# Interleaved first loads with matmuls on ones ahead of them, and a last pair of output tiles worked by token halves with the final norm beside it

## The reference

```python
# first block: norm, one wide projection
xn = x * rsqrt(mean(x*x) + 1e-6) * norm_w
h = xn @ w_in
...
# last layer of the second block: attention, then SwiGLU, then the final norm
x = x + window_attn_mixer(...)
gu = rmsnorm(x, norm_ffn_w[1]) @ ffn_w_in[1]
x = x + (silu(gate) * up) @ ffn_w_out[1]
return x * rsqrt(mean(x*x) + 1e-6) * norm_final_w
```

## Time and profile before

| | |
|---|---|
| device time, median of 3 runs | 1524.91 us (1524.15 to 1524.92) |
| the profiled execution | 1526.1 us, of which the span of its instructions is 1524.3 us |
| PE busy | 1467.6 us (96% of the span), 7120 instructions |
| DVE, ACT, POOL busy | 833.8, 581.1, 37.8 us |
| DMA | 123.02 MB, mean 81 GB/s |

### The profile page before, as it was taken

One profiled execution on the slowest core, in us unless ns is written; L12 is line 12 of the kernel. 1 busy time (PEld: TensorE's weight loads), 2 busy tenths in 40 slices (PEclk: granted clock), 3 DMA queues, 4 the chain that ended last, 5 costly groups with the idle time before them and its releaser, 6 DMA issues.

```text
span 1524.3 us, 18003 instructions
## 1 busy us (share of the span) xinstructions
PE 1467.6 (96%) x7120; PEld 1199.6 (79%) x7120; DVE 833.8 (55%) x1592; ACT 581.1 (38%) x1032; POOL 37.8 (2%) x43
## 2 busy tenths in 40 slices
PE   6999998999999899999999999999899999999996
PEld 6778795789788678888888887867678888888885
DVE  5677756567645764544345455587755443344433
ACT  5555533354433443322223233366654232222221
POOL 0011000000000000000000000000000000000000
PEclk9999997999999999999999999999999999999998
DMA  6221120032121112222322223210012222322221
GB/s 220 70 83 56 56 83 28 14 116 79 56 83 56 56 59 107 83 93 78 123 107 83 86 83 128 83 56 1 29 55 93 102 86 84 121 94 100 84 81 70
DMA packets 20899, 123.02 MB, mean 81 GB/s; under 512 B 2256, under 2 KB 2896, under 8 KB 9680
## 3 DMA queue, kind: packets, MB, share of 16 engines
q1 hardware_dynamic: 20816, 121.89, 23.2%
HBM read 119.78 MB, written 2.10 MB: 80 GB/s over the span
## 4 chain that ended last, share of the span: by engine, by line
PE 62%; issue 25%; DVE 8%; ACT 4%; DMA 0%; POOL 0%; DVEq 0%; POOLq 0%; SPq 0%; ACTq 0%
PE PS L231 57%; PE PS L246 3%; PE PS L254 2%; DVE WL L219 1%; DVE FT L227 1%; DVE FT L219 1%; ACT FR L206 1%; DVE FR L219 1%; ACT FT L206 1%; ACT WH L206 1%; DVE G L219 1%; DMA RAW<-in_w_in 0%; DVE FT L223 0%; DVE FP L227 0%; DVE STR L227 0%
## 5 line engine op out<-in xcount | busy, mean ns | idle before, releaser
L231 PE MATMUL PS<-XH,WH 128*128 128x512 f32 x1080 | 428.7, 397 | 0.0
L231 PE MATMUL PS<-XH,WL 128*128 128x512 f32 x1080 | 422.1, 391 | 0.0
L231 PE MATMUL PS<-XL,WH 128*128 128x512 f32 x1080 | 421.9, 391 | 0.0
L231 PE MATMUL PS<-FR,WH 128*128 128x512 f32 x1088 | 342.6, 396 | 12.5 <-DVE FR L219 4.8
L219 DVE TENSOR_TENSOR WL<-RAW,WH 128x1024 fp32r<-128x1024 f32 (+2 forms) x242 | 263.2, 1129 | 153.8 <-ACT WH L206 152.9
L206 ACT ACTIVATE WH<-RAW 128x1024 fp32r<-128x1024 f32 (+2 forms) x242 | 223.9, 974 | 141.6 <-PE PS L231 135.0
L231 PEld LDWEIGHTS PS<-FR,WH 128*128 128x128 f32 x1088 | 204.0, 190 | 60.8 <-issue 9.9
L231 PEld LDWEIGHTS PS<-XH,WH 128*128 128x128 f32 x1080 | 203.6, 189 | 48.6 <-issue 7.5
L231 PEld LDWEIGHTS PS<-XH,WL 128*128 128x128 f32 x1080 | 203.4, 188 | 43.4
L231 PEld LDWEIGHTS PS<-XL,WH 128*128 128x128 f32 x1080 | 203.7, 189 | 40.6 <-issue 0.5
L231 PE MATMUL PS<-FR,WL 128*128 128x512 f32 x544 | 214.0, 393 | 0.0
(11 more groups left out here) (114 smaller groups left out, 1274.5 us busy)
## 6 DMA issues: line engine op xcount, KB each, us to landing
RAW<-in_f_in SPq DMA_DIRECT2D x44, 1024.0 KB, 4.8
RAW<-in_w_in SPq DMA_DIRECT2D x13, 1024.0 KB, 4.8
RAW<-in_m_in SPq DMA_DIRECT2D x12, 1024.0 KB, 4.9
RAW<-in_f_oa SPq DMA_DIRECT2D x16, 768.0 KB, 4.3
RAW<-in_f_ob SPq DMA_DIRECT2D x16, 640.0 KB, 3.8
RAW<-in_a_in SPq DMA_DIRECT2D x6, 1024.0 KB, 5.0
RAW<-in_w_out SPq DMA_DIRECT2D x4, 1024.0 KB, 4.9
RAW<-in_m_out SPq DMA_DIRECT2D x4, 1024.0 KB, 4.8
```

Of the source, the lines that this page charges most:

```text
L231: f = lambda e: e.matmul(o, l, r, start=start, stop=stop, skip_group_check=True)
```

## The change

**At the start.** Weight chunk 0 now comes in four pieces of 256 KB, each issued right behind a piece of x of 512 KB. Of the small constants only the eight columns of `norm_w` (4 KB, `n1`) are issued early, the rest (`sm`, 166 KB) behind the last piece. `prep_all` writes out the split of a weight piece and then those of its two x tiles, four times. `warm_up` gives PE 16 matmuls of 128 columns on the tile `ONE` before anything else; their result is not used.

**At the end.** The pairs dp = 0 to 2 are as before. The last pair is `last_pair`: the products for tokens 0 to 255 of both output tiles (66 matmuls of 256 columns), the norm for these tokens, then the same for tokens 256 to 511. Tiles 0 to 5 are multiplied by the final norm weight ahead of that, on ACT, into `G`; tiles 6 and 7 follow by halves. DVE then multiplies four tiles at once by 1/rms (128x4x256), in place, and each such product leaves by one DMA of 512 KB.

```diff
     xv = A["xT"].rearrange("(k p) s -> p k s", p=128)
-    t_sm = load(SM[:, :], A["small"], "sm")
-    t_x = [load(XT[:, 2 * i:2 * i + 2, :], xv[:, 2 * i:2 * i + 2, :], f"x{i}") for i in range(1)]
...
     def w_load(j):
         ap, nk, wdt = chunks[j]
         dst = RAW[:, j % 2, 0:nk * wdt]
         after = w_split[j - 2][-1] if j >= 2 else None
-        if j == 0:
-            half = nk * wdt // 2
-            SP.add(lambda e: e.dma_start(dst[:, 0:half], ap[:, 0:half]), [], (wd[0], 16), 1.5)
-            WHEN[wd[0], 16] = SP.t + 2.0
-            return
-        tok = (wd[j % 2], 16 * (j // 2 + 1))
+        tok = (wd[j % 2], 16 * ((j + 1) // 2))
         SP.add(lambda e: e.dma_start(dst, ap), [after], (wd[j % 2], 16), 3.0)
         WHEN[tok] = SP.t + 2.0
 
-    def w_prep(j, halves=(0, 1)):
...
-        for a, b in [((0, n0), (n0, nk))[i] for i in halves]:
+        for a, b in ((0, n0), (n0, nk)):
             r = RAW[:, j % 2, a * wdt:b * wdt]
-            here = w0b if j == 0 and a else (wd[j % 2], 16 * (j // 2 + 1))
-            toks.append(split(r, WH[:, j % 2, a * wdt:b * wdt], WL[:, j % 2, a * wdt:b * wdt], here, free))
-        if 1 not in halves:
-            w_part[j] = toks
-            return
+            toks.append(split(r, WH[:, j % 2, a * wdt:b * wdt], WL[:, j % 2, a * wdt:b * wdt],
+                              (wd[j % 2], 16 * ((j + 1) // 2)), free))
...
-        n0 = (nk + 1) // 2
-        return j, h, l, [w_split[j][0 if k < n0 else 1] for k in range(nk)]
-    w_load(0)
-    t_x += [load(XT[:, 2 * i:2 * i + 2, :], xv[:, 2 * i:2 * i + 2, :], f"x{i}") for i in range(1, 2)]
-    w0b = load(RAW[:, 0, 1024:2048], chunks[0][0][:, 1024:2048], "w0b")
-    t_x += [load(XT[:, 2 * i:2 * i + 2, :], xv[:, 2 * i:2 * i + 2, :], f"x{i}") for i in range(2, 4)]
+        return j, h, l, [w_split[j][k * len(w_split[j]) // nk] for k in range(nk)]
+    t_x, t_w0, t_n1 = [], [], None
+    for i in range(4):
+        part = slice(512 * i, 512 * i + 512)
+        t_x.append(load(XT[:, 2 * i:2 * i + 2, :], xv[:, 2 * i:2 * i + 2, :], f"x{i}"))
+        t_w0.append(load(RAW[:, 0, part], chunks[0][0][:, part], f"w0{i}"))
+        if i == 0:
+            t_n1 = load(SM[:, 0:8], A["small"][:, 0:8], "n1")
+    t_sm = load(SM[:, 8:NSMALL], A["small"][:, 8:NSMALL], "sm")
     w_load(1)
     w_at[0] = 2
     t_co = load(CO[:, :], A["const"], "co")
...
     def prep_parts(d, wcol):
         w = SM[:, wcol + d:wcol + d + 1]
         x = XT[:, d, :]
-        h = copy(XH[:, d, :], x, st["x"][d], t_sm, st["xfree"], scale=w)
-        l = stt(XL[:, d, :], x, w, XH[:, d, :].bitcast(F32), ALU.mult, ALU.subtract, h, st["x"][d], t_sm, st["xfree"])
+        tw = t_n1 if wcol == C_N1 else t_sm
+        h = copy(XH[:, d, :], x, st["x"][d], tw, st["xfree"], scale=w)
+        l = stt(XL[:, d, :], x, w, XH[:, d, :].bitcast(F32), ALU.mult, ALU.subtract, h, st["x"][d], tw, st["xfree"])
         xs[d] = [h, l]
 
...
+    def warm_up():
+        b, fb = bank.take()
+        for i in range(16):
+            t = mm(PS[:, b, 0:128], ONE[:, :], ONE[:, :], True, True, t_one, fb, last=(i == 15))
+        bank.put(b, t)
     def prep_all(wcol):
-        w_prep(0, (0,))
-        for d in range(KT):
-            prep_parts(d, wcol)
-            if d == 2:
-                w_prep(0, (1,))
+        w_split[0] = []
+        for i in range(4):
+            part = slice(512 * i, 512 * i + 512)
+            w_split[0].append(split(RAW[:, 0, part], WH[:, 0, part], WL[:, 0, part], t_w0[i]))
+            prep_parts(2 * i, wcol)
+            prep_parts(2 * i + 1, wcol)
         for d in range(KT):
             prep_square(d)
...
             if half == 1:
                 st["xfree"] = tu
-            for dp in range(4):
+            for dp in range(3 if half == 1 and next_w == C_FIN else 4):
...
+            if half == 1 and next_w == C_FIN:
+                last_pair(hid)
+                return
             for hh, hl, tk in hid:
                 fr.put(hh, t)
                 fr.put(hl, t)
 
+    def last_pair(hid):
+        YT, oo = G, out.rearrange("(k p) s -> p k s", p=128)
+        cw = lambda d: SM[:, C_FIN + d:C_FIN + d + 1]
+        tm = [copy(YT[:, d, :], XT[:, d, :], st["x"][d], t_sm, st["g", d], scale=cw(d)) for d in range(6)]
+        ws = [w_use(), w_use()]
+        bs = [bank.take(), bank.take()]
+        bn = [bank.take() for _ in range(2)]
+        sq = [ft.take() for _ in range(2)]
+        so = dsem("out")
+        for th in range(2):
+            c = slice(256 * th, 256 * th + 256)
+            done = []
+            for u, (b, fb) in enumerate(bs):
+                for k in range(FH):
+                    j, h, lo, wt = ws[k // 6]
+                    hh, hl, tk = hid[k]
+                    t = mm3(PS[:, b, c], (h[:, k % 6, u * 128:u * 128 + 128], lo[:, k % 6, u * 128:u * 128 + 128]),
+                            (FR[:, hh, c], FR[:, hl, c]), k == 0, k == FH - 1, wt[k % 6], tk, fb, last=(k == FH - 1))
+                done.append(t)
+            (b, fb), rc, m = bn[th], sc(2), sc(2)
+            cols2 = [slice(c.start + 128 * i, c.start + 128 * i + 128) for i in range(2)]
+            for i in range(2):
+                mm(PS[:, b, i:i + 1], ACC[:, cols2[i]], ONE[:, 0:1], i == 0, False, st["acc"], fb, t_one, last=False)
+            for u in range(2):
+                d = 6 + u
+                x = XT[:, d, c]
+                tx = tt(x, x, PS[:, bs[u][0], c], ALU.add, done[u], st["x"][d], xs[d])
+                q, qf = sq[u]
+                t2 = act(FT[:, q, c], x, ACT.Square, tx, qf)
+                tm.append(copy(YT[:, d, c], x, tx, t_sm, st["g", d], scale=cw(d)))
+                for i in range(2):
+                    t = mm(PS[:, b, i:i + 1], FT[:, q, cols2[i]], ONE[:, 0:1], False, u == 1, t2, last=(u == 1 and i == 1))
+            t = ts(m, PS[:, b, 0:2], 1.0 / D, ALU.mult, t, s2=EPS, op1=ALU.add)
+            t = rpow(rc, m, 2, t)
+            for i in range(2):
+                t2 = tr(PS[:, b, 128 + 128 * i:256 + 128 * i], rc[:, i:i + 1].to_broadcast([128, 128]), IDN, t, t_co, last=(i == 1))
+            r = PS[:, b, 128:384].unsqueeze(1).to_broadcast([128, 4, 256])
+            for p in range(2):
+                y = YT[:, 4 * p:4 * p + 4, c]
+                t3 = tt(y, y, r, ALU.mult, t2, tm)
+                SP.add(lambda e, y=y, p=p, c=c: e.dma_start(oo[:, 4 * p:4 * p + 4, c], y), [t3], (so, 16))
...
+    warm_up()
     prep_all(C_N1)
...
     ffn(1, C_FIN)
-    norm_col()
-    rc = st["rc"]
-    b, fb = bank.take()
-    t = spread(b, lambda i: rc[:, i:i + 1].to_broadcast([128, 128]), st["rct"], fb)
-    oo = out.rearrange("(k p) s -> p k s", p=128)
-    so = dsem("out")
-    for d in range(KT):
-        f, ff = ft.take()
-        t1 = stt(FT[:, f, :], XT[:, d, :], SM[:, C_FIN + d:C_FIN + d + 1], PS[:, b, :], ALU.mult, ALU.mult, t, st["x"][d], ff)
-        SP.add(lambda e, d=d, f=f: e.dma_start(oo[:, d, :], FT[:, f, :]), [t1], (so, 16))
     assert w_next[0] == len(chunks)
 
     with nc.Block() as block:
         @block.sync
         def _(e):
             SP.play(e, sems)
-            e.wait_ge(sems["out"], 16 * KT)
+            e.wait_ge(sems["out"], 16 * 4)
 
         @block.scalar
         def _(e):
```

More of the change, by code:

```diff
@@ L312, in blocks_kernel @@
     w_done = [None] * len(chunks)
-    w_at, w_part = [0], {}
+    w_at = [0]
     def w_load(j):
@@ L318, in w_load, with w_prep @@
         after = w_split[j - 2][-1] if j >= 2 else None
-        if j == 0:
-            half = nk * wdt // 2
-            SP.add(lambda e: e.dma_start(dst[:, 0:half], ap[:, 0:half]), [], (wd[0], 16), 1.5)
-            WHEN[wd[0], 16] = SP.t + 2.0
-            return
-        tok = (wd[j % 2], 16 * (j // 2 + 1))
+        tok = (wd[j % 2], 16 * ((j + 1) // 2))
         SP.add(lambda e: e.dma_start(dst, ap), [after], (wd[j % 2], 16), 3.0)
         WHEN[tok] = SP.t + 2.0
-    def w_prep(j, halves=(0, 1)):
+    def w_prep(j):
         while w_at[0] < min(j + 2, len(chunks)):
@@ L335, in w_prep @@
         ap, nk, wdt = chunks[j]
-        toks = w_part.pop(j, [])
+        toks = []
         n0 = (nk + 1) // 2
         free = w_done[j - 2] if j >= 2 else None
-        for a, b in [((0, n0), (n0, nk))[i] for i in halves]:
+        for a, b in ((0, n0), (n0, nk)):
             r = RAW[:, j % 2, a * wdt:b * wdt]
-            here = w0b if j == 0 and a else (wd[j % 2], 16 * (j // 2 + 1))
-            toks.append(split(r, WH[:, j % 2, a * wdt:b * wdt], WL[:, j % 2, a * wdt:b * wdt], here, free))
-        if 1 not in halves:
-            w_part[j] = toks
-            return
+            toks.append(split(r, WH[:, j % 2, a * wdt:b * wdt], WL[:, j % 2, a * wdt:b * wdt],
+                              (wd[j % 2], 16 * ((j + 1) // 2)), free))
         w_split[j] = toks
```

## The result

| | before | changed |
|---|---|---|
| median | 1524.75 us (1524.15 to 1525.26, 6 runs) | 1529.9 us (1525.99 to 1531.29, 6 runs) |
| ratio | | 1.0032, 95% interval 1.0022 to 1.0042 |
| span of the profiled execution | 1524.3 us | 1529.5 us |
| mean granted clock, profiled | 0.985 | 0.982 |

The changed kernel is slower by 0.3%, some 5 us. Its chunk "a1" starts earlier by what was forecast; its last pair is longer by more than that.

What follows compares the result with a forecast made beforehand. PE, busy 96% of the span, was taken as the bound, leaving gains only before its first and after its last matmul. Start -3.3, last pair +4.4, clock +2.4 gave +3.5 us: 1528.4 us, range 1524.5 to 1531.5.

Steps and rivals of the forecast that it cites:

- The start: First weight chunk and x: smaller, reordered pieces let chunk "a1" start at 23.1 instead of 26.38, gaining 3.3 us.
- third rival: At the start, PE and not DVE ends last, so the warm-up brings 2.0 us on top: 1526.4 us, chance 0.08.
- From 26.38 on the queues stand in the same order as before: After the start, later waits are on work that moves along, so the 3.3 us gain carries to the end.
- The wait for "ob": Last pair: six ACT copies ahead of the split of weight chunk "ob" make PE wait 5.0 us.
- rival "faster": Last pair: the six copies don't stand in the way, so PE's wait and the slow spells go: 1521.0 us, chance 0.06.
- The border norm: Between the last pair's halves: PE waits out the first half's whole norm, 3.0 us.
- The end chain: After the last matmul: the second half's norm chain up to the products takes 3.35 us, where it was 5.87.
- Products and output: End of the kernel: two products of 1024 columns and two DMAs take 6.2 us, allowing for slower 1 KB rows.
- The clock: Last pair: PE's matmuls run at half clock after both new waits, +2.4 us, bounds 0 and 4.6.
- Part of the slow time falls into the wait: Last pair: reason for charging the slow spell after the first wait, of 5.0 us, at only 1.1 us.
- The spell at the border: Last pair: half clock after the 3.0 us wait between the token halves, taken as 1.3 us.

Runs made afterwards that it cites:

- e4: Changed kernel without the 16 warm-up matmuls: 1530.03 us, ratio 1.0029 to the kernel before.
- e8: e7 without the 16 warm-up matmuls: 1521.97 us, ratio 0.9976 to the kernel before.
- e3: Changed kernel with the six copies into G moved behind the split of the last weight chunk: 1523.42 us, ratio 0.9988 to the kernel before.
- e6: e5 with both tiles' matmuls on chunk "oa" ahead of those on "ob" in each half: 1523.52 us, ratio 0.9983 to the kernel before.
- e9: e6 with the first half's sums and transposes placed between the second half's matmuls, ahead of those on "ob": 1520.07 us, ratio 0.9972 to the kernel before.
- e10: e9 with the start of e7: 1518.31 us, ratio 0.9958 to the kernel before.
- e1: Changed kernel's start with the old end (no last_pair): 1519.95 us, ratio 0.9966 to the kernel before.
- e7: Changed start, old end, chunk 1 split ahead of the squares, norm_col and first evictions behind two tiles of "a1": 1520.08 us, ratio 0.9956 to the kernel before.
- e12: e10 timed again without edit, on the same chip as e11: 1517.82 us, ratio 0.9958 to the kernel before.
- e11: e7 timed again without edit, on the same chip as e12: 1520.74 us, ratio 0.9966 to the kernel before.
- e5: e3 with the first half's sums and transposes spread among the second half's matmuls, in separate banks: 1525.01 us, ratio 0.9991 to the kernel before.
- e2: Kernel before, with its old start, given the changed end (last_pair): 1533.0 us, ratio 1.005 to the kernel before.

## Why the prediction came out as it did

The forecast was 1528.4 us, with a chance of 0.5 for more than 0.2% slower; measured 1529.9, 0.3% slower. In its own steps:

- **The start.** Right for "a1": 23.13 against 23.1, and right on the way: 13.45 against 13.5 for the last weight piece, 16.38 against 16.4 for the additions. The first large matmul came at 7.79 instead of 8.8, as the first piece was there at 5.5 and not 6.6; that changed nothing, since DVE ends last. That the warm-up is worth nearly nothing is shown by e4. The 2.0 us of the third rival were worked out from 22 slow matmuls; e4 and e8 have 13.
- **"From 26.38 on the queues stand in the same order as before", so the gain is carried to the end.** Only partly. Tile 5's addition is 2.94 us earlier than before (1495.66, that is 0.20 behind the pair's start; the forecast was 3.3), but on the way there the lead was less: PE now idles 1.34 us before the sums, and the stretch behind it is slow in every profile with this start and norm order (0.71 here), in none with the old start. By the first 512-column matmul 3.25 us had become 1.77 (36.62 against 38.39). The step had priced the 0.8 us that `norm_col` takes, not the slow stretch behind it. That 1.2 us of the lead came back in the middle, where the changed kernel's profile is shorter by as much (below), is luck: no term of the prediction has it, and no run shows why.
- **The wait for "ob".** Right in place, cause and size: 4.86 for 5.0. e3 shows the cause by removing it. What the prediction had wrong is what would be left without the copies: it took the wait to go wholly, and 1.2 us stayed, from the halved width and the order of the tiles (e6, with the other order, has no such wait). Its rival "faster", at 1521.0, also took the slow spell at the border to be gone; e3 has the copies out of the way and is 1523.42, since 1.18 us of wait and the border's slow spell stayed.
- **The border norm.** 3.2 for 3.0. **The end chain** 3.2 for 3.35. **Products and output** 5.8 for 6.2 (1523.67 to 1529.5); no row stood behind the part of the 6.2 that was for rows of 1 KB. Together the work of the pair is about 4.1 us longer, with 4.4 forecast.
- **The clock.** The mis-sized term: +2.4 forecast. The 48 matmuls took 8.34 us for 5.7, the 66 took 9.24 for 7.9: 2.6 and 1.4, 4.0 in all. It lies inside the bounds of 0 to 4.6. "Part of the slow time falls into the wait" was the error: the clock in the stretch that is mostly wait is 0.92, and 0.66 in the one behind it. By an estimate from these two rows that is 1.1 us of half clock in the wait and 5.7 us on the matmuls behind it. The spell at the border, taken as 1.3, cost 1.4.

Sum: -2.9 for -3.3, +4.1 for +4.4, +4.0 for +2.4: +5.2 on the profiled execution where +3.5 was forecast.

**What stays open.** A single kernel scatters by several us from one execution to the next (before: 1523.19 to 1529.2 in 20 runs; e3: 1519.47 to 1526.75 in 12), and much of it arises in code that no edit touched. The windows show how, e9 first and then e10, over the same 60 us of the span (e10 is some 3 us further on in the program there):

```profile
403.00:463.00 60.00, 55.83 (x286) 47.79 (x287) 34.87 (x90) 24.70 (x51) 2.28 (x4) 0.94 0.16 53
```

```profile
403.00:463.00 60.00, 57.84 (x314) 50.12 (x313) 36.95 (x94) 24.73 (x49) 2.28 (x4) 1.00 0.17 55
```

PE issues 286 matmuls at a mean clock of 0.94, or 314 at 1.00. Part of the 28 is only the different place. The clock is not: windows of 20 us show two spells of half clock in e9 between 360 and 440 us behind its first 512-column matmul, and none in e10. From the first 512-column matmul to the last load of an `f_in` chunk it is 1273.9 us in before, 1272.7 in the changed kernel and in e9, 1268.9 in e1, 1274.9 in e7 and 1269.2 in e10. The granted clock accounts for most of this: summed over that stretch in windows of 20 us, the time at half clock is by an estimate 38 us in before, in the changed kernel and in e7, 35 in e9, 27 in e1, e10 and e12, and 42 in e11. The stretch less half of that time is 1253.0 to 1255.7 us in all 14 profiles. So part of e1's 5 us, against a lead of 2.6 at that matmul, is such time, and so is most of the 6 us by which e7's profile lost to e1's there. An early start does not decide it: e7, e10, e11 and e12 have the same start and middle, and the time at half clock is 38, 27, 42 and 27 us. Why an execution draws more or fewer of these stretches, and whether a kernel's median is shifted by them, 14 profiles don't settle.

## What to carry to other kernels

Before putting work "beside" other work, list what stands behind it in the queue of its engine: six copies of 0.6 us, useful and harmless by themselves, cost 6 us because a weight split stood behind them, and in e5 and e6 products of 2.35 us did the same to the last additions. Halving tiles makes every operand wanted in half the time or less, so look again at each load and split that was just in time. A gain of PE's first matmul is none while another engine ends the stage, and the same warm-up that brings nothing in one order brings 1 us in another.

## What the runs showed of the hardware

- After idle times of PE of 1.34 us (start, with 1.05 us of one-column matmuls behind it) and 4.86 us (last pair), and behind the border of 3.17 us, matmuls ran at half clock for a time: the granted clock was 0.71, 0.66 and 0.82 on average over the stretches behind them. All seven profiles with the first of these waits (1.34 to 1.53 us) have the slow stretch. After the 1.18 us in e3 there was none.
- PE's first matmuls without a warm-up stand 0.21 us apart, 22 of them in before and 13 in e4 and e8. The clock column of the windows reads 1.00 there all the same, so that this is half clock is read from the spacing alone.
- Sixteen float32 matmuls of 128 columns on ones stand as 32 records and take 6.63, 5.71 and 5.36 us in three profiles of the same code.
- The same loads land up to 1.3 us apart between executions: ACT had the second weight piece at 9.61 in e11 and at 8.31 in e12, of the same start. The old start's first matmul was at 11.86 in before and at 11.12 in e2.
- A product of 128x4x256 with an operand from PSUM took 1.18 us (two in 2.35), and two of them with 1 MB of output in rows of 1 KB were through 5.8 us after the first began.
